# Re-ordered gate/up turns in a two-layer encoder: alternating PSUM banks, accumulating DMAs that read DRAM, half-MB loads

## What is computed

```
def swiglu(x, wg, wu, wd):
    return (jax.nn.silu(x @ wg) * (x @ wu)) @ wd
...
        h = h + swiglu(rmsnorm(h, ffn_norm[layer]), w_gate[layer], w_up[layer], w_down[layer])
```

## Time and profile before

| What | us |
|---|---|
| median of 3 runs (lowest to highest) | 1651.67 (1651.43 to 1651.87) |
| profiled execution, first to last instruction (its span; no other time of it is given) | 1649.6 |
| median less that span | 2.1 |
| turns of layer 0 | from 91.0 to 499 |
| turns of layer 1 | from 1006.0 to 1413.8 |

### The profile page before, as it was taken

One profiled execution on the slowest core, in us unless ns is written; L12 is line 12 of the kernel. 1 busy time (PEld: TensorE's weight loads), 2 busy tenths in 40 slices (PEclk: granted clock), 3 DMA queues, 4 the chain that ended last, 5 costly groups with the idle time before them and its releaser, 6 DMA issues.

```text
span 1649.6 us, 19819 instructions
## 1 busy us (share of the span) xinstructions
PE 1639.0 (99%) x7456; PEld 1351.4 (82%) x7456; DVE 1433.4 (87%) x1604; ACT 1137.2 (69%) x1596; POOL 128.4 (8%) x164
## 2 busy tenths in 40 slices
PE   9999999999999999999999999999999999999998
PEld 8888888888888888888777888888888888888887
DVE  7889999999999899777676868999999999888867
ACT  6677777777767755556665566777777776676653
POOL 1100000000000000002010000000000000000000
PEclk9999999999999999999999999999999999999999
DMA  8578888888887886845434557888888888887883
GB/s 297 176 216 259 265 258 259 259 260 257 261 258 228 257 268 191 281 177 180 153 128 154 179 182 201 255 257 257 258 259 260 259 260 258 284 241 243 230 255 148
DMA packets 179063, 384.67 MB, mean 233 GB/s; under 512 B 7316, under 2 KB 7444, under 8 KB 178840
## 3 DMA queue, kind: packets, MB, share of 16 engines
q1 hardware_dynamic: 162832, 324.67, 56.6%
q0 software_dynamic: 15840, 57.68, 18.4%
q10 hardware_dynamic: 296, 1.06, 0.2%
HBM read 323.61 MB, written 2.10 MB: 197 GB/s over the span
## 4 chain that ended last, share of the span: by engine, by line
PE 96%; DVE 2%; DMA 1%; SPq 0%; issue 0%; ACT 0%
PE acc L1798 9%; PE acc L1799 9%; PE acc L1800 9%; PE acc L1811 8%; PE acc L1812 8%; PE acc L1813 8%; PE acc L1675 6%; PE acc L1677 6%; PE acc L1676 6%; PE acc L1905 6%; PE acc L1903 6%; PE acc L1904 6%; PE acc L1888 3%; PE acc L1890 3%; PE acc L1889 3%; DMA raw<-pool_w_in 1%
## 5 line engine op out<-in xcount | busy, mean ns | idle before, releaser
L1269 DVE TENSOR_TENSOR w_lo<-raw,w_hi 128x1024 fp32r<-128x1024 f32 x440 | 524.7, 1216 | 36.2 <-ACT w_hi L792 29.9
L792 ACT ACTIVATE w_hi<-raw 128x1024 fp32r<-128x1024 f32 x440 | 459.6, 1059 | 133.6 <-PE acc L1800 77.5
L850 ACT ACTIVATE w_hi<-raw 128x1024 fp32r<-128x1024 f32 x221 | 234.0, 1061 | 158.6 <-PE acc L1905 120.6
L1441 DVE TENSOR_TENSOR w_lo<-raw,w_hi 128x1024 fp32r<-128x1024 f32 x221 | 266.3, 1221 | 58.1 <-ACT w_hi L850 52.3
L1799 PE MATMUL acc<-w_lo,xT_hi 128*128 128x512 f32 x640 | 249.0, 389 | 0.0
L1800 PE MATMUL acc<-w_hi,xT_lo 128*128 128x512 f32 x640 | 249.0, 389 | 0.0
L1798 PE MATMUL acc<-w_hi,xT_hi 128*128 128x512 f32 x640 | 249.0, 389 | 0.0
L1903 PE MATMUL acc<-w_hi,hT_hi 128*128 128x512 f32 x456 | 177.5, 389 | 0.1
L1904 PE MATMUL acc<-w_lo,hT_hi 128*128 128x512 f32 x456 | 177.4, 389 | 0.0
L1905 PE MATMUL acc<-w_hi,hT_lo 128*128 128x512 f32 x456 | 177.4, 389 | 0.0
L1800 PEld LDWEIGHTS acc<-w_hi,xT_lo 128*128 128x128 f32 x640 | 120.1, 188 | 25.0
(11 more groups left out here) (204 smaller groups left out, 2802.0 us busy)
## 6 DMA issues: line engine op xcount, KB each, us to landing
raw<-w_gate_in SPq DMA_DIRECT2D x88, 1024.0 KB, 7.3
raw<-w_up_in SPq DMA_DIRECT2D x88, 1024.0 KB, 5.3
raw<-w_down_in SPq DMA_DIRECT2D x88, 1024.0 KB, 6.9
raw<-raw POOLq DMA_DIRECT2D x110, 512.0 KB, 5.3
raw<-w_q_in SPq DMA_DIRECT2D x16, 1024.0 KB, 5.1
raw<-w_o_in SPq DMA_DIRECT2D x16, 1024.0 KB, 5.1
raw<-w_kv_in SPq DMA_DIRECT2D x4, 1024.0 KB, 6.7
raw<-pool_w_in SPq DMA_DIRECT2D x3, 1024.0 KB, 13.9
```

The source lines that it names most:

```text
L792: nc.scalar.activation(w_hi[:, (before + n) % RING, :], raw[:, slot, off:off + 2 * C], ACT.Copy).then_inc(hi_ready, 1)
L1269: nc.vector.tensor_tensor(w_lo[:, w, :], weight_half(unit), w_hi[:, w, :].bitcast(F32), ALU.subtract).then_inc(unit_ready, 1)
L1441: nc.vector.tensor_tensor(w_lo[:, LAP_DOWN[l].ring(n), :], src, w_hi[:, LAP_DOWN[l].ring(n), :].bitcast(F32), ALU.subtract).then_inc(unit_ ...
```

## The change

- `SUM_ORDER` is a new order of the same 22 units: B11, B11, gate 4, gate 5, T1, T1, B21, B21, B22, B22, T2, T2, gate 6, T3, T3, gate 7, up 4, T4, up 5, T4, up 6, up 7.
- The products accumulate in four PSUM banks (`gate0`, `gate1`, `up0`, `up1`), one set of banks in even turns and the other in odd turns. Four times in a turn ScalarE copies a bank (`chain_copy`), and TensorE goes on in that bank behind a wait for the copy. VectorE's part is one `gate_add` and one `up_add` of 1024 columns, both in the next turn. The five combining operations at the end of the turn are gone. `act_lo` moves to unit 0 of the turn after the next, `sum_silu` to behind unit 2, the `quad_move` parts to units 16 to 21, `act_hi` to unit 21.
- B11 is rounded with scale -1, and its rest is made by a scalar_tensor_tensor.
- B12 is not loaded. The accumulating DMAs read it from DRAM: T1 is B12 added onto B11's half slot, T3 is B12 added onto B22's. The T3 DMA also waits for T2.
- The loads are 512 KB, into ten half slots that a plan (`TurnsPlan`) gives out: 14 a turn in place of eight of 1 MB.

```diff
-SUM_ORDER = [("B11", 0), ("B11", 1), ("B21", 0), ("gate", 4), ("B21", 1), ("gate", 5), ("B22", 1), ("T1", 1),
-             ("B22", 0), ("T1", 0), ("gate", 6), ("gate", 7), ("T3", 0), ("T2", 1), ("T4", 0), ("T2", 0), ("T4", 1),
-             ("up", 5), ("T3", 1), ("up", 4), ("up", 6), ("up", 7)]
+SUM_ORDER = [("B11", 0), ("B11", 1), ("gate", 4), ("gate", 5), ("T1", 0), ("T1", 1), ("B21", 0), ("B21", 1),
+             ("B22", 0), ("B22", 1), ("T2", 0), ("T2", 1), ("gate", 6), ("T3", 0), ("T3", 1), ("gate", 7),
+             ("up", 4), ("T4", 0), ("up", 5), ("T4", 1), ("up", 6), ("up", 7)]
...
+T_SUMS = {("T2", 0): 5, ("T2", 1): 7, ("T4", 0): 12, ("T4", 1): 15}
...
+class TurnsPlan:
...
+        self.free = [n + 1 - UD for n in range(2 * RING)] + [-2 * UD] * 2
...
+                half = min(range(HALVES), key=lambda one: (self.free[one], one))
...
+            def load_sum_turns(l):
+
+                for one in TURNS.pieces:
+                    if one.ready > -2 * UD:
+                        sp.wait_ge(unit_ready, sum_units(l, 1) + one.ready)
...
@@ ScalarE, sum_turn @@
-                    nc.scalar.activation(w_hi[:, (before + n) % RING, :], raw[:, slot, off:off + 2 * C],
-                                         ACT.Copy).then_inc(hi_ready, 1)
-                    if n == 0 and j > 1:
+                    else:
+                        ac.wait_ge(half_in[TURNS.of[j, form, s].half], 16 * half_loads(l, j, form, s))
+                    nc.scalar.activation(w_hi[:, (before + n) % RING, :], raw_half(j, form, s), ACT.Copy,
+                                         scale=-1.0 if form == "B11" else 1.0).then_inc(hi_ready, 1)
+                    if n == 2 and j > 1:
                         sum_silu(l, j - 1)
-                    if n == 4:
-
-                        ac.wait_ge(unit_used, before + AT["B11", 1] + 1)
-                        ac.wait_ge(job_out, 2 * j + JOB_GU[l])
-                        nc.scalar.activation(common[:, 0, :], acc[:, P1, :], ACT.Copy).then_inc(p1_copied, 1)
+                    if n == 6:
+                        ac.wait_ge(quad_full, turned + 1)
+                        chain_copy(l, j, ("B11", 1), act[:, 0, :], up1, -1.0)
+                    if n == 8:
+                        chain_copy(l, j, ("T1", 1), common[:, 1, :], up0)
+                    if n == 14:
+                        chain_copy(l, j, ("T2", 1), common[:, 0, :], up1)
+                    if n == 17:
+                        ac.wait_ge(quad_full, turned + 2)
+                        chain_copy(l, j, ("T3", 1), act[:, 1, :], up1, -1.0)
                     if j < NFB - 1:
-                        for part in {7: (0,), 8: (1,), 10: (2,), 11: (3, 4), 14: (5,), 17: (6, 7)}.get(n, ()):
+                        for part in {16: (0, 1), 18: (2,), 19: (3, 4), 20: (5, 6), 21: (7,)}.get(n, ()):
                             quad_move(l, j - 1, part)
-                        if n == 19:
+                        if n == 21:
                             act_hi(l, j - 1)
...
@@ VectorE, sum_turn @@
+                    if n == 0 and j > 1:
+                        act_lo(l, j - 2)
+                    if n == 1 and j > 1:
+                        gate_add(l, j - 1)
                     if n == 3:
                         if j > 1:
+                            up_add(l, j - 1)
                             common_out(l, j - 1)
                         else:
                             up_out(l, j - 1)
+                    if n == 4:
                         quad_turn(l, j - 1, 0)
-                    if n == 5:
+                    if n == 11:
                         quad_turn(l, j - 1, 1)
...
+                    for one in T_ORDER:
+                        if T_SUMS[one] == n:
+                            weight_sum(l, j, *one)
...
@@ TensorE, sum_turn @@
+                    if form == "T2" and s == 0:
+                        te.wait_ge(chain_copied, 4 * c + 1)
+                    if form == "B22" and s == 0:
+                        te.wait_ge(chain_copied, 4 * c + 2)
+                    if form == "T3" and s == 0:
+                        te.wait_ge(chain_copied, 4 * c + 3)
+                    if form == "up" and s == 4:
+                        te.wait_ge(chain_copied, 4 * c + 4)
...
@@ GpSimd, turn_sums @@
-                        gp.wait_ge(raw_in[SLOT_U[s]], 16 * sum_loads(l, j, "up", s))
-                        gp.dma_start(half("T1", s), half("T3", s), accum_op=ALU.add).then_inc(t1_in[s], 16)
...
+                        b12 = up_v[l][:, 4 * s:4 * s + 2, cols]
                         gp.wait_ge(unit_ready, before + AT["B11", s] + 1)
+                        gp.dma_start(raw_half(j, "T1", s).rearrange("p (k n) -> p k n", k=2), b12,
+                                     accum_op=ALU.add).then_inc(t1_in[s], 16)
...
+                        gp.wait_ge(unit_ready, before + AT["B22", s] + 1)
+                        gp.wait_ge(t_sum, sum_done(l, j, ("T2", s)))
+                        gp.dma_start(raw_half(j, "T3", s).rearrange("p (k n) -> p k n", k=2), b12,
+                                     accum_op=ALU.add).then_inc(t3_in[s], 16)
```

More of the change, by code:

```diff
@@ L82 @@
 SUM_STEPS = SUM_UNITS * SUM_TURNS
[L85 to L98, removed]
@@ new lines, with __init__ @@
+T_ORDER = sorted(T_SUMS, key=T_SUMS.get)
+LINKS = [("B11", 1), ("T1", 1), ("T2", 1), ("T3", 1)]
+SLOTS = RING + 1
+HALVES = 2 * SLOTS
+PLACE = {"B11": "B11", "T1": "B11", "T2": "B11", "B21": "B21", "T4": "B21", "B22": "B22", "T3": "B22",
+         "gate": "gate", "up": "up"}
+@dataclass
+class Piece:
+    half: int
+    nth: int
+    ready: int
+    first: int
+    turn: int
+    form: str
+    n: int
+class TurnsPlan:
+    def __init__(self):
+        life = {}
+        for unit in SUM_ORDER:
+            life.setdefault((PLACE[unit[0]], unit[1]), []).append(AT[unit])
+        for s in range(SUM_SETS):
+            life["B11", s].append(T_SUMS["T4", s] + 1)
+            life["B22", s].append(T_SUMS["T2", s])
+        self.free = [n + 1 - UD for n in range(2 * RING)] + [-2 * UD] * 2
+        self.count = [0] * HALVES
+        self.of, self.pieces = {}, []
+        for j in range(1, NFB):
+            for key in sorted(life, key=lambda key: min(life[key])):
+                half = min(range(HALVES), key=lambda one: (self.free[one], one))
+                self.count[half] += 1
+                start = SUM_UNITS * (j - 1)
+                piece = Piece(half, self.count[half], self.free[half], start + min(life[key]), j, *key)
+                self.free[half] = start + max(life[key]) + 1
+                self.of[j, *key] = piece
+                self.pieces.append(piece)
+        self.pieces.sort(key=lambda one: (one.ready, one.first))
@@ L179, in __init__ @@
                 needs.setdefault((pair, "sum", 1, 4 * n_set), []).append(n)
-        self.free = [one - SUM_UNITS for one in SLOT_LAST]
+        self.free = [max(TURNS.free[2 * i:2 * i + 2]) - SUM_STEPS for i in range(SLOTS)]
         count = [0] * SLOTS
@@ L486, in sum_units, with half_loads, raw_half, turn_banks @@
             return (LAP_GU[l] + 2).units(SUM_UNITS * (j - 1))
[L488 to L493, removed]
+        def half_loads(l, j, form, n):
+            one = TURNS.of[j, form, n]
+            return TURNS.count[one.half] * l + one.nth
+        def raw_half(j, form, n):
+            half = TURNS.of[j, PLACE[form], n].half
+            return raw[:, half // 2, half % 2 * 2 * C:(half % 2 + 1) * 2 * C]
         def sum_done(l, j, unit):
-            return len(T_SUMS) * (SUM_TURNS * l + j - 1) + T_SUMS.index(unit) + 1
+            return len(T_ORDER) * (SUM_TURNS * l + j - 1) + T_ORDER.index(unit) + 1
+        def turn_banks(l, j):
+            gate, up = (2 * (JOB_GU[l] % 2), 2 * ((JOB_GU[l] + 1) % 2)) if j % 2 == 0 else (4, 6)
+            return gate, gate + 1, up, up + 1
         def out_after(l, b):
@@ L781, in sum_turn @@
                     form, s = unit
-                    slot, off = turn_half(form, s)
-                    if turn_load(unit) not in landed:
-                        landed.add(turn_load(unit))
-                        ac.wait_ge(raw_in[slot], 16 * sum_loads(l, j, *turn_load(unit)))
                     if form == "T1":
```

218 lines of the change are left out of this document (87 added, 131 removed).

## The result

The changed kernel takes **1931.33 us** (median of 4 runs, 1929.09 to 1935.0), beside 1651.55 of the kernel before in the same session: a ratio of 1.170 (95% interval 1.1683 to 1.1716), a loss of 280 us where 68 were forecast. The direction was right; the time lies far above the range (1675 to 1768).

What follows compares the result with a forecast made beforehand. PE bounds the kernel, 40.80 us a turn for 180 matmuls; a loop through VectorE, the T3 DMA and ScalarE makes turns 44.7. The loss of 68.7 takes the span from 1649.6 to 1718.3, plus 2.1 gives 1720 us; range 1675 to 1768.

Steps and rivals of the forecast that it cites:

- no engine's sum over the turn: Each engine's work in a turn stays under 40.80 us: VectorE about 36.0 plus 0.2, ScalarE 33.9, DMAs 78%.
- the chain that the prediction named: In a turn, VectorE's front, the T3 DMA and ScalarE's tail follow one another: 44.7 us instead of 40.80.
- The stall at unit 13: PE waits for ScalarE's copy of T2's bank, which ends at 24.9 against PE's 24.26: 0.65 us in turn 2.
- The nothing for the down product: `gate_add` and `up_add` there are covered by its own first units: no loss, 2 us should the cover go.
- The nothing for the loads: The half-MB loads are issued at least seven units (9.5 us) ahead of their readers and cost nothing.
- the stall at the front: Early in a turn, PE waits at units 4 to 8 for VectorE's `w_lo` and loses 2.5 us.
- the DMAs' sum: DMA share of a turn falls from 85% to 78%: loads about 21 us, the four accumulating DMAs 10.9.
- the loop: From `hi` 0 through `lo` 9, the T3 DMA and ScalarE's tail to the next `hi` 0: period 38.6 + L.
- L: Time from the end of `lo` 9, when the second T3 DMA is issued, to its landing: taken as 6.1 us.
- the forecast's sum: Turn 2 of a layer loses 3.15 us, turns 3 to 10 lose 3.9 each: 34.4 a layer, 68.7 in both.
- stays whole: Turn 1 of a layer, without `gate_add`, `sum_silu` or `act_lo` in its front, loses nothing.
- slow accumulation: Rival: T3's accumulation from DRAM takes 8.4 us, period 47.0, 1762 us; at 10.5 about 1800; chance 0.15.

Runs made afterwards that it cites:

- Runs 1 to 3: Room for GpSimd's DMA descriptors: changed kernel at 2048, 1766.28 us; kernel before with only T1's DMAs reading B12 from DRAM, 1726.31 at 1024, 1652.96 at 2048.
- run 8: The kernel of run 7 with the old room for GpSimd's DMA descriptors, 1024 instead of 2048: 1899.03 us, ratio 1.151.
- run 7: The kernel of run 1 with a new unit order and the bank copies, quads, `act_lo`, `act_hi`, `sum_silu` and T4's sums moved: 1697.14 us.
- run 1: The changed kernel with room for GpSimd's DMA descriptors (`dynamic_dma_scratch_size`) 2048 instead of 1024: 1766.28 us, ratio 1.070.
- run 10: The kernel of run 7 with one B21 unit ahead of T1 and T2's and T4's sums and the quads shifted: 1688.16 us, ratio 1.0225.
- run 4: The kernel of run 1 with `act_lo` moved from unit 0 to unit 16 and `sum_silu` one unit later: 1783.91 us, ratio 1.0805.

## Why the prediction was right and wrong

**Right: nothing to win, and no engine's sum over the turn.** PE had no idle time in a turn, and the sums of VectorE and ScalarE came out as worked out (36.55, 33.29). That such sums don't decide was right too: the time is in a chain, and in the chain that the prediction named. The stall at unit 13, behind the copy of T2's bank, stands where it put it, and ScalarE waits for T3 ahead of unit 14; of the four copies PE waits for this one alone. The nothing for the down product held: by their starts the turns lost 284 us, which is the whole 283.6 of the span. The nothing for the loads held as well: ScalarE's waits for DMAs in the turns are T1's 141.3 us and T3's 181.4.

**Right by luck: the stall at the front.** It was put at units 4 to 8 and stands at unit 5, but not for VectorE's queue: ScalarE waits there for T1's second DMA, in the first turn of each layer too. With room the stalls there are 0.6 us at most.

**Wrong without harm: the DMAs' sum.** 78% of 40.80 is 31.9 us; measured are 36.6 of the 16 engines' time. Loads have 43.3% of the turn, 23.7 us (forecast about 21), and the four accumulating DMAs 23.9%, 13.1 us (10.9, "taken the same with a DRAM source").

**Right: the parts of the loop that are engine work.** `hi` 0 starts at -4.90 (forecast -4.56), `lo` 4 ends 8.11 after the turn's start (8.60), both in turn 5 of after; with room, `lo` 8 ends at 15.5 (16.1), and the way from T3's landing to the next `hi` 0 takes 17.0 to 17.6 in the turns of its loop (16.85). The 1024-wide scalar_tensor_tensor is no dearer than a plain one (1.22 busy, 1.14 to the next start where it was taken for 1.20).

**The step that failed: L.** The prediction said "the second T3 is issued about 1.2 us behind the first and shares the engines with it", and that it would "land like T1 after 4.8, sharing adds" 1.5. Two things in it were wrong.

- *The issue.* The second DMA was not issued behind the first but behind its landing. In turn 4 of after `lo` 9 ends at 273.19 (the second of the four of 1.135 us from 270.92), and the second T3 lands at 284.66: L is 11.5, not 6.1; in turn 5, where that DMA itself took 8.4, it was 13.9. Runs 1 to 3 and run 8 against run 7 settle that it is the room: 165, 73 and 202 us hang on that one number. The rows that could have warned were the earlier trace rows: 576 packets for 2.10 MB is 3.6 KB each, and the change halves the length of a row.
- *The size.* The first DMA of a pair, from DRAM, lands after 5.7 to 6.3 us, not 4.8, and the second of a T3 pair after 7.2 to 8.4 where the room lets it follow at once. By itself this puts L at 7.9 and the period at 46.4, which is run 1. The trace of before could have shown half of it: the earlier trace rows has both DMAs of each T3 pair in one row. Taken apart, the first of the 20 pairs there landed after 4.8 to 8.6 us and the second, issued 0.6 behind, after 6.7 to 10.5 with a median of 7.8, so that no second was as quick as the 6.1 taken for L. With an L of 7.9 the forecast's sum would have been 2 x (3.15 + 8 x 5.6), some 96 us, of the 115 of run 1 (111 by the span of the profiled run). Of the other 15 turn 2 has 6.3: the prediction has 3.15 for it, and run 1 shows 46.3 and 48.0. Turns 3 to 10 have 4.8 more, and the first turns 3.9: a first turn "stays whole" in the prediction and takes 42.7 and 42.8, since there too the second T3 comes too late for the copy at unit 13. In the changed kernel the first turns take 52.9 and 52.4.

**The sum of a turn, by the prediction's own terms.** It had 17.2 (`lo` 9) + 6.1 (L) + 16.85 (to the next `hi` 0) + 4.56 = 44.7. Turn 4 of after has 20.4 + 11.5 + 17.9 + 4.9 = 54.7. So 5.4 of the 10 us between them come from T3's L; 3.2 from T1, whose second DMA is held just as long and delays `lo` 5 to 13.6 and with it `lo` 9; 1.0 from the way to `hi` 0 (the slower matmuls, it seems: run 1 with its faster clock has 17.0 to 17.6 there; no run took the clock apart); and 0.3 from the start. A T1 DMA that comes too late was not in any of the cases.

**The rival that came nearest** was slow accumulation: it has "the second behind the first whole", with 8.4 for L and 1762. It named what happened, and priced it with 4.8 a DMA instead of about 6, for T3 alone, so that it came out 170 us low; it had a chance of 0.15, and the range ended just above it. Its price of 10.5, "about 1800", was nearer, and stood outside the range. The trace of before could not show the hold, since its pairs are issued together; what was missing was the question of how two DMAs of twice the rows get issued at all.

**TensorE's clock** was no step of the prediction. The lower level made 4.4 us a turn of PE's busy time, but by the sum above at most about 1 us a turn of it was on the loop: PE is late there anyway, and the next turn hangs on ScalarE and VectorE. With the stalls gone the clock comes back: its mean is 0.945 in the changed kernel, 0.991 in run 1 and 0.999 in run 10.

## What to carry to other kernels

When the source or shape of a DMA that GpSimd issues changes, count its rows as well as its bytes (that the rows did it is argued here, the room is shown), and look whether two of them can still be out at once: an idle time of GpSimd that ends with "issue", or just when an earlier DMA of its lands, is the sign. Engine sums under the bound show only that a plan can work; whether it does is decided by the longest loop through the engines and the DMAs, and its DMA terms need the time of the second of a pair, not the median of all. And a DMA that is let go sooner may land later, as T1's second did in run 4.

## What the runs showed of the hardware

- GpSimd did not issue a second 256-row DMA, at a room of 1024, until the first had landed: in all 40 pairs of the changed kernel it went out 0.26 to 0.34 us after that, 5.1 us idle each. At 2048 the pairs of run 1 went out 1.2 to 2.7 us apart. All of these DMAs read DRAM.
- Issuing one took 1.21 us of GpSimd for 256 rows from DRAM, and 0.86 for 128 rows from `raw` (medians of T1 in after and before).
- Accumulating 512 KB from DRAM took 5.7 to 6.3 us as the first of a pair in the changed kernel and in run 1, 7.2 to 8.4 as the second of a T3 pair 1.2 us apart in run 1, and up to 11.0 as T1's second in run 10. The second T3 of the changed kernel, issued after the first had landed, took 5.8 to 6.3 in 17 of 20 pairs and 7.0 to 8.4 in three. By the Trainium skill, page "DMA: Bandwidth & Descriptors", section "Anatomy of one DMA", a GpSimd DMA of 512 KB would take an estimated 3.2 us; the section does not speak of accumulating ones, and none here was that quick.
- In turn 4 of after, PE's matmuls ran 0.43 us apart behind its waits of 3.8 and 5.7 us (granted clock 0.52 behind the second, to 290.80), then 0.23 apart again (1.00); the granted clock of the whole turn was 0.91.
